# Memory query made turned at the head of the gate stage, another order of the first normed tiles, and the last output row by thirds

## The chip, the cores and the metric

The kernel runs on one core of a Trainium2 chip. The metric is the device time of one execution in microseconds (us). The engines are named as in the profile: PE (TensorE), with PEld its weight loads, DVE (VectorE), ACT (ScalarE), POOL (GpSimd), and SP (SyncE), which here only issues DMAs.

## The reference

One layer of a hybrid decoder for 1024 new-sequence tokens (`S`) and 8 sample tokens (`NB`), `T` = 1032 in all, width 1024. All is float32.

```
z = rmsnorm(x, norm1_g) @ w_in      # split: qa, ka, va (3 groups), qm, km, vm, om, gates, ga, gb
qm = qm * 64 ** -0.5                # the memory query, 512 columns
o_att = windowed, dilated attention of the groups (1, 4, 16), merged by their log-sum-exp
h_m   = mLSTM over chunks of tokens (qm, km, vm, input and forget gates), with a matrix state
x = x + (sigmoid(ga) * (o_att @ w_att_out) + sigmoid(gb) * ((sigmoid(om) * h_m) @ w_m_out)) @ w_o
y = x + (silu(h @ w_gate) * (h @ w_up)) @ w_down,   h = rmsnorm(x, norm2_g)
```

Besides y the outputs are the new key and value caches and the memory's states, for the sequence and for the samples (the latter from attention over their caches and one step of the memory).

## The kernel before

Every product is made of three, of high and low parts of both operands (`products`), as fp32r. `w_in` is taken in pieces of 128 rows by 512 columns: SP loads a piece into one of three `raw` buffers, POOL makes the high part `whi` and the low part `wlo` in a ring of 15 places, and the next load of a buffer waits for the low part. The first eight pieces are rounded by ACT (`round_weights`).

The program is a chain of blocks; each engine has a queue of its own in every block.

1. `project`: first the tokens are normed in tiles of 128 (`NormInput`): squares and root on ACT, the inverse on DVE, spread over the partitions by PE (`pe_norm`), then DVE scales the transposed tile in halves (`nrm`), ACT rounds it (`hi`) and DVE takes the rest (`lo`). `Projection` runs over 13 kinds of 512 columns (`KINDS`), nine units each: eight tiles of tokens (24 products of 128x512) and the samples' unit (16 products). A step u of all engines handles unit u and the tails of those before. Queries and keys are turned by PE two units later, copied by ACT, and stored by SP (`m_tr` and `a_tr`). Attention of group g takes two items for a tile of tokens (`Attention.at` says at which step), with products ahead of the softmax (`qk`), transposes and the products behind it (`pv`). `SampleScores`, from step `late` on, loads a cache tile and a query per step and reduces them on DVE; SP loads one step ahead.
2. `gate_projections`: 16 units of 128 gate columns by 1032 tokens, made already turned (weights stationary), in three segments of 344 tokens each (`segment_product`); ACT takes a segment into `sg` and stores a unit. From segment i = 3 (`FIRST`) on, `Chunks` runs the memory over eight chunks of tokens, five steps each, between the segments. `sp_init` loads the first two chunks.
3. `layer_end`: the output products, and the feed-forward part `Ffn`. Its last loop adds the products of `w_down` to `acc`, a row m of 128 columns at a time; PE turns a finished row (`turn`), ACT and DVE copy its halves, SP stores them. After the last row PE turns the new tokens' columns, and ACT and SP store them.

The order within a block is written out by hand. A block ends with an exit at the line of its `with` (L1139, L2248).

Of the kernel before, what the change touches and what calls it, by code (L numbers as in the profile page):

```python
# [12 lines left out]
F32 = mybir.dt.float32  # L13
# [5 lines left out]
P = 128  # L19
D = 1024  # L20
S = 1024
NB = 8
# [31 lines left out]
KINDS = [(0, 2), (0, 0), (1, 2), (0, 1), (1, 0), (1, 1), (2, 0), (2, 1), (2, 2)] + [("m", x) for x in range(4)]  # L54
# [60 lines left out]
def weight_pieces(t):  # L115
# [3 lines left out]
    cols += [CGA, CGA + 512, CGB, CGB + 512, COM, COM + 512]  # L119
# [251 lines left out]
class NormInput:  # L371
# [79 lines left out]

    def act_root(self, n):

# [5 lines left out]
        if n == 0:  # L459
            act.wait_ge(self.one, 1)  # L460
# [3 lines left out]
                       accum_out=self.ssq[0:rows, n:n + 1]).then_inc(self.sqd, 1)  # L464
        act.wait_ge(self.var, n + 1)
        act.activation(self.ssq[0:rows, n:n + 1], self.ssq[0:rows, n:n + 1], ACT.Sqrt).then_inc(self.std, 1)

    def act(self, n):
# [4 lines left out]
        rows, cols = self.rows(n), self.cols(n)  # L473
        for v in self.halves(n):
            act.wait_ge(self.nrm, v + 1)
            act.activation(core.xs[v % 2][:, 0, :, cols],
                           self.tmp[:, v % 2, :].rearrange("p (k c) -> p k c", k=4)[:, :, 0:rows],
                           ACT.Copy).then_inc(self.hi, 1)
# [21 lines left out]
    def dve(self, n):  # L500

        dve, core, ch = self.core.nc.vector, self.core, self.core.dve
        if not self.valid(n):
            return
        rows, cols = self.rows(n), self.cols(n)
        if n == 0:
            dve.memset(self.ssq[:], 1.0).then_inc(self.one, 1)
            dve.memset(core.hs[:].bitcast(F32), 0.0).then_inc(self.zero, 1)
        root = self.ssq[0:rows, n:n + 1]
        dve.wait_ge(self.sqd, n + 1)  # L510
        dve.tensor_scalar(root, root, 1.0 / D, EPS, ALU.mult, ALU.add).then_inc(self.var, 1)
        dve.wait_ge(self.std, n + 1)
        dve.reciprocal(root, root).then_inc(self.inv, 1)
        if n == 0:
            dve.wait_ge(self.g_in, 16)
# [3 lines left out]
        at = (n % 4) * P  # L519
        ch.link(dve.tensor_copy(self.rs[:, 0:rows], core.ps[:, 7, at:at + rows]))  # L520
        for v in self.halves(n):
            if v >= 2:
                dve.wait_ge(self.lo, v - 1)
            for k in range(4):
# [4 lines left out]
                if k < 3:  # L529
                    ch.mark(ins)  # L530
                else:
                    ch.wait()
                    ins.then_inc(self.nrm, 1)
# [3192 lines left out]
```

## Time and profile before

| | |
|---|---|
| median of 3 runs | 2161.61 us (2161.17 to 2162.16) |
| the profiled execution | 2158.37 us, span 2156.6 us |
| PE busy | 2117.9 us, 98% |
| PEld, DVE, ACT, POOL busy | 1977.4, 1066.8, 631.7, 715.7 us |
| DMA | 365.17 MB, mean 169 GB/s |
| median landing of a weight load of w_in, 256 KB | 4.2 us |
| median landing of a store of gates, 516 KB | 3.8 us |

A row of the timeline is start, duration, engine, line, operation, output<-input, and in brackets how long the engine was idle before and what ended that. A duration of a PE product includes its way through the array: products start closer together than that. SPq and ACTq rows are DMA issues.

### The profile page before, as it was taken

What the parts mean: (1) busy time and instruction counts of PE and PEld (TensorE: products, weight loads), DVE (VectorE), ACT (ScalarE), POOL (GpSimd) and SP (SyncE); (2) the same over time, 40 slices, a digit from 0 to 9 for tenths busy, and PEclk for the clock granted to TensorE, in tenths of its full rate; (3) what the DMA queues carried; (4) which work ended last, traced back from release to release, by engine and by line L of the source; (5) the groups of instructions that cost most, each with busy time, mean ns of one, the idle gap of its engine ahead of it and who ended that gap; (6) DMA issues with size and microseconds to landing.
All of it is one profiled execution on the core that took longest, in us unless ns stands there. A gap on an engine that the chain in (4) does not pass through costs nothing.

```text
span 2156.6 us, 36189 instructions
## 1 busy us (share of the span) xinstructions
PE 2117.9 (98%) x14248; PEld 1977.4 (92%) x14248; DVE 1066.8 (49%) x2112; ACT 631.7 (29%) x1354; POOL 715.7 (33%) x636
## 2 busy tenths in 40 slices
PE   7999999999999999999999999999999999999999
PEld 6788899999877778999989999999999999999998
DVE  5675777775233341233266544398454454442212
ACT  5221465544233232333211011143332332221001
POOL 3433321232112222222052334224544544554310
PEclk9999999999999999999999999999999999999999
DMA  6625534355548834545467641415545545387712
GB/s 201 210 101 170 176 117 144 131 187 174 180 154 286 271 132 149 165 148 162 134 214 239 207 154 54 148 60 180 183 150 178 182 151 178 105 329 288 259 41 79
DMA packets 233735, 365.17 MB, mean 169 GB/s; under 512 B 39222, under 2 KB 134262, under 8 KB 230870
## 3 DMA queue, kind: packets, MB, share of 16 engines
q1 hardware_dynamic: 211534, 317.48, 44.3%
q10 hardware_dynamic: 22032, 45.38, 6.1%
q8 instruction: 113, 1.85, 0.3%
q14 instruction: 56, 0.46, 0.1%
HBM read 276.19 MB, written 174.68 MB: 209 GB/s over the span
## 4 chain that ended last, share of the span: by engine, by line
PE 52%; DVE 5%; issue 2%; DMA 1%; ACT 1%; SPq 0%; DVEq 0%; ACTq 0%
PE ps L2855 20%; PE ps L2199 17%; PE ps L366 4%; PE ps L367 4%; PE ps L368 4%; PE ps L1637 1%; DMA h_mem<-c_ht 1%; DVE acc L3126 1%; PE ps L1412 0%; DVE x_a L2549 0%; PE ps L1629 0%; PE ps L1620 0%; PE ps L1646 0%; DVE x_c L2549 0%; DVE misc L3102 0%
## 5 line engine op out<-in xcount | busy, mean ns | idle before, releaser
L341 POOL CAST whi<-raw 128x512 fp32r<-128x512 f32 x228 | 167.6, 735 | 1046.1 <-PE ps L682 431.0
L343 POOL TENSOR_TENSOR wlo<-raw,whi 128x512 fp32r<-128x512 f32 x231 | 323.3, 1400 | 34.6 <-issue 10.3
L366 PE MATMUL ps<-whi,x_a 128*128 128x512 f32 x416 | 178.6, 429 | 0.0
L736 ACT ACTIVATE zt<-ps 128x512 f32<-128x512 f32 x104 | 62.1, 597 | 356.6 <-PE ps L368 302.6
L367 PE MATMUL ps<-wlo,x_a 128*128 128x512 f32 x416 | 166.5, 400 | 0.0
L368 PE MATMUL ps<-whi,x_a 128*128 128x512 f32 x416 | 166.5, 400 | 0.0
L366 PE MATMUL ps<-whi,x_b 128*128 128x512 f32 x416 | 166.0, 399 | 0.0
L368 PE MATMUL ps<-whi,x_b 128*128 128x512 f32 x416 | 166.0, 399 | 0.0
L367 PE MATMUL ps<-wlo,x_b 128*128 128x512 f32 x416 | 165.9, 399 | 0.0
L2855 PE MATMUL ps<-x_a,whi 128*128 128x258 f32 x960 | 156.2, 285 | 2.0 <-DVE acc L2657 1.8
L2855 PE MATMUL ps<-x_c,whi 128*128 128x258 f32 x960 | 154.5, 283 | 0.5 <-DVE acc L3334 0.5
L2199 PE MATMUL ps<-x_a,whi 128*128 128x344 f32 x792 | 148.2, 323 | 3.2 <-DVE x_a L2549 1.3
L3060 POOL TENSOR_TENSOR wlo<-wlo_f,whi 128x512 fp32r<-128x512 f32 x88 | 122.1, 1410 | 57.4 <-issue 39.1
L2855 PEld LDWEIGHTS ps<-x_a,whi 128*128 128x128 f32 x960 | 133.4, 191 | 2.6 <-DVE acc L2657 2.0
L2199 PEld LDWEIGHTS ps<-x_a,whi 128*128 128x128 f32 x792 | 129.0, 189 | 5.2 <-issue 5.1
L2855 PEld LDWEIGHTS ps<-x_c,whi 128*128 128x128 f32 x960 | 132.3, 190 | 0.8 <-issue 0.7
L3589 DVE TENSOR_TENSOR acc<-acc,ps 128x1032 f32<-128x1032 f32 x32 | 39.3, 1229 | 171.6 <-PE ps L2199 171.6
L982 DVE CUSTOM_DVE_ANT_0 sc<-ps,misc 128x128 f32<-128x128 f32 (+1 forms) x192 | 56.0, 348 | 120.9 <-PE ps L933 93.0
L368 PEld LDWEIGHTS ps<-whi,x_a 128*128 128x128 f32 x416 | 103.9, 250 | 10.4
L368 PEld LDWEIGHTS ps<-whi,x_b 128*128 128x128 f32 x416 | 103.5, 249 | 10.3
L367 PEld LDWEIGHTS ps<-wlo,x_b 128*128 128x128 f32 x416 | 103.4, 249 | 10.2
L366 PEld LDWEIGHTS ps<-whi,x_b 128*128 128x128 f32 x416 | 103.5, 249 | 9.9
(416 smaller groups left out, 4930.1 us busy)
## 6 DMA issues: line engine op xcount, KB each, us to landing
out<-in_cache_kv_w SPq DMA_DIRECT2D x144, 512.0 KB, 6.3
raw<-in_w_in SPq DMA_DIRECT2D x147, 256.0 KB, 4.2
a_tr<-tt SPq DMA_DIRECT2D x48, 256.0 KB, 2.0
out<-in_cache_kv_w SPq DMA_DIRECT2D x24, 508.0 KB, 5.5
raw<-in_w_down SPq DMA_DIRECT2D x44, 256.0 KB, 6.0
gates<-e_sg ACTq DMA_DIRECT2D x16, 516.0 KB, 3.8
rw<-gates ACTq DMA_DIRECT2D x16, 516.0 KB, 4.7
out<-zt SPq DMA_DIRECT2D x26, 256.0 KB
```

The lines of the kernel that those rows point to most:

```text
L341: pool.tensor_copy(self.whi[:, self.place(p), :], raw).then_inc(self.w_hi, 1)
L343: pool.tensor_tensor(self.wlo[:, self.place(p), :], raw, self.whi[:, self.place(p), :].bitcast(F32), ALU.subtract).then_inc(self.w_lo, 1)
L366: nc.tensor.matmul(out, lhs[0], rhs[0], start=start, stop=False)
L367: nc.tensor.matmul(out, lhs[0], rhs[1], start=False, stop=False)
L368: return nc.tensor.matmul(out, lhs[1], rhs[0], start=False, stop=stop)
L736: act.activation(self.zt[:, u % Z, :], ps[:, u % 2, :], ACT.Copy, scale=self.scale(u)).then_inc(self.ev, 1)
L982: ins = dve.tensor_tensor_reduce(self.sc[:, W % 2, 2 * par + j, 0:span], ps[:, 3 + par, 2 * j * P:2 * j * P + span], mask, SCALE, 3 * NEG, ...
L1637: last = pe.matmul(ps[:, bank, at], self.ww[:, self.at(h), :], self.v[:, b, h, :], start=True, stop=True)
L2199: last = nc.tensor.matmul(ps[0:m, bank + s, 0:SEG], w, x[:, s * SEG:(s + 1) * SEG], start=(k == 0 and i == 0), stop=(k == nk - 1 and i == 2))
L2855: last = core.nc.tensor.matmul(core.ps[:, bank + s, 0:Q], a, b[:, s * Q:(s + 1) * Q], start=start and i == 0, stop=stop and i == 2, skip_g ...
L3060: pool.tensor_tensor(core.wlo[:, at, :], self.source(c, x), core.whi[:, at, :].bitcast(F32), ALU.subtract).then_inc(core.a_lo, 1)
L3589: dve.tensor_tensor(seg3(acc[:, m, :]), seg3(acc[:, m, :]), self.res(n, m), ALU.add).then_inc(self.add[0], 1)
```

## The change

- The kind ("m", 0), the memory's query, leaves `KINDS` (12 kinds stay). Its columns stand first among the pieces of the gate stage, which has `U` = 20 units: four of the query (`QUERY`), copied with the scale, then the 16 of the gates. A query unit is stored by ACT with two DMAs: the tokens' part to `m_tr[0]` and the new tokens' part to `zm_s`, whose rows are tokens, so that each number goes to a place of its own. `FIRST` is 15 instead of 3. The first two chunks are loaded at i = 13, after SP has waited for all query stores.
- Group 2 of attention takes one item in each unit (before, two in three units). `late` is 78 instead of 81.
- At the start ACT makes a Sqrt of a constant, then the squares of tile 0 ahead of the first rounding; squares of tile 1, rounding and normed halves follow in another order, and DVE's order is written out in `dve_start`.
- The last row of the output is made in three segments of tokens, each with its own bank, addition and transposes; the row before is turned between them, as are the new tokens' columns, whose store goes ahead of the last row's.

```diff
-KINDS = [(0, 2), (0, 0), (1, 2), (0, 1), (1, 0), (1, 1), (2, 0), (2, 1), (2, 2)] + [("m", x) for x in range(4)]
+KINDS = [(0, 2), (0, 0), (1, 2), (0, 1), (1, 0), (1, 1), (2, 0), (2, 1), (2, 2)] + [("m", x) for x in range(1, 4)]
...
-    cols += [CGA, CGA + 512, CGB, CGB + 512, COM, COM + 512]
+    cols += [CQM, CGA, CGA + 512, CGB, CGB + 512, COM, COM + 512]
...
+    def act_first(self):
+
+
+        act = self.core.nc.scalar
+        act.wait_ge(self.one, 1)
+        act.activation(self.rs[:, 0:1], self.ssq[:, NT:NT + 1], ACT.Sqrt)
...
+    def act_square(self, n):
 
         act, core = self.core.nc.scalar, self.core
         if not self.valid(n):
             return
         rows, cols = self.rows(n), self.cols(n)
         act.wait_ge(self.x_in[n], 16)
-        if n == 0:
-            act.wait_ge(self.one, 1)
         spare = (core.xs[0][:, :, :, cols].rearrange("p a k c -> p (a k) c") if n < NT else
                  self.x[0:NB, 0, :].rearrange("p (k c) -> p k c", k=KD))
         act.activation(spare, self.rows_of(n).rearrange("p (k c) -> p k c", k=KD), ACT.Square,
...
+    def act_half(self, n, v):
+
+        act, core, rows = self.core.nc.scalar, self.core, self.rows(n)
+        act.wait_ge(self.nrm, v + 1)
+        act.activation(core.xs[v % 2][:, 0, :, self.cols(n)],
+                       self.tmp[:, v % 2, :].rearrange("p (k c) -> p k c", k=4)[:, :, 0:rows],
+                       ACT.Copy).then_inc(self.hi, 1)
...
+    def dve_start(self):
+
+
+        dve = self.core.nc.vector
+        dve.memset(self.ssq[:], 1.0).then_inc(self.one, 1)
+        dve.memset(self.core.hs[:].bitcast(F32), 0.0).then_inc(self.zero, 1)
+        self.dve_var(0)
+        self.dve_inverse(0)
+        dve.wait_ge(self.g_in, 16)
+        self.dve_factor(0)
+        self.dve_normed(0, 0)
+        self.dve_var(1)
+        self.dve_normed(0, 1)
+        self.dve_inverse(1)
+        self.dve_rest(0, 0)
+        self.dve_rest(0, 1)
+        self.dve_block(1)
...
-            return [core.m_tok[n, :, x - 1, :]] if x else []
+            return [core.m_tok[n, :, x - 1, :]]
...
+                at = g * (self.ITEMS + self.TAIL) + j
+                self.at[proj.unit(1, 0, 0) + (at * 3 // 2 if g < 2 else at + self.ITEMS + self.TAIL)] = (g, j)
         self.loads = {}
...
-        late = proj.unit("m", 0, 0)
+        late = proj.unit("m", 1, 0) - 3
...
+            norm.act_first()
+            norm.act_square(0)
             core.round_weights(0)
+            norm.act_sqrt(0)
+            norm.act_square(1)
             core.round_weights(1)
-            norm.act_root(0)
-            for p in range(2, 5):
+            core.round_weights(2)
+            norm.act_half(0, 0)
+            norm.act_sqrt(1)
+            norm.act_half(0, 1)
+            core.round_weights(3)
+            core.round_weights(4)
+            norm.act_keep(0)
+            core.round_weights(5)
+            norm.act(1)
+            for p in range(6, FIRST):
                 core.round_weights(p)
-            norm.act(0)
-            norm.act_root(1)
-            for p in range(5, FIRST):
-                core.round_weights(p)
-            norm.act_keep(0)
-            norm.act(1)
             norm.act_keep(1)
...
         def _(dve):
-            norm.dve(0)
-            norm.dve(1)
+            norm.dve_start()
...
-        self.load(0)
-        self.load(1)
...
-    U = 2 * KD
-    FIRST, PER, WIDE = 3, 6, 3
-    LOADS = {9: 0, 15: 1, 21: 2}
+    U, QUERY = 2 * KD + 4, 4
+    FIRST, PER, WIDE = 15, 6, 3
+    LOADS = {9: 0, 21: 1, 27: 2}
     p0 = core.taken
-    core.taken += 4 * KD
...
+        def stored(u):
+
+
+            return 16 * (u // 2) + 16 * min(u // 2, QUERY // 2)
+
         @block.sync
         def _(sp):
             chunks.sp_init()
             for i in range(3 * U):
                 core.load_weights(piece(i))
+                if i == FIRST - 2:
+                    for x in range(2):
+                        sp.wait_ge(out[x], stored(QUERY + x))
+                    chunks.load(0)
+                    chunks.load(1)
...
-                if i == FIRST:
+                if i == 3:
...
-                    act.wait_ge(out[u % 2], 16 * (u // 2))
+                    act.wait_ge(out[u % 2], stored(u))
                 wait_segment(core, act, i, p0, mm)
-                act.activation(sg[:, u % 2, s * SEG:(s + 1) * SEG], ps[:, i % 2, 0:SEG], ACT.Sigmoid).then_inc(ev, 1)
+                part = sg[:, u % 2, s * SEG:(s + 1) * SEG]
+                if u < QUERY:
+                    act.activation(part, ps[:, i % 2, 0:SEG], ACT.Copy, scale=SCALE).then_inc(ev, 1)
+                else:
+                    act.activation(part, ps[:, i % 2, 0:SEG], ACT.Sigmoid).then_inc(ev, 1)
                 if s == 2:
                     act.wait_ge(ev, i + 1)
-                    act.dma_start(core.gates[u], sg[:, u % 2, :]).then_inc(out[u % 2], 16)
+                    if u < QUERY:
+                        act.dma_start(core.m_tr[0, :, :, u * P:(u + 1) * P].rearrange("n p c -> p n c"),
+                                      sg[:, u % 2, 0:S].rearrange("p (n c) -> p n c", n=NT)).then_inc(out[u % 2], 16)
+                        with core.nc.allow_non_contiguous_dma(reason="queries of the new tokens"):
+                            act.dma_start(core.zm_s[:, u * P:(u + 1) * P].rearrange("b c -> c b"),
+                                          sg[:, u % 2, S:T]).then_inc(out[u % 2], 16)
+                    else:
+                        act.dma_start(core.gates[u - QUERY], sg[:, u % 2, :]).then_inc(out[u % 2], 16)
                 if step(i) is not None:
                     chunks.act(step(i))
             for i in range(2):
-                core.defer(out[i], 16 * U // 2)
+                core.defer(out[i], stored(U))
...
-            for half, done in enumerate((self.ya, self.yv)):
-                sp.wait_ge(done, k + 1)
+            if k == KD - 1:
+                sp.wait_ge(self.yn, 1)
+                sp.dma_start(o[1].rearrange("b s d -> (b s) d"), self.new).then_inc(self.new_out, 16)
+            for half in (0, 1) if k < KD - 1 else (1, 0):
+                sp.wait_ge((self.ya, self.yv)[half], k + 1)
                 sp.dma_start(y[k, half], self.turned(k, half).rearrange("p (n c) -> p n c", c=P)).then_inc(
                     self.out[k % 2], 16)
-        sp.wait_ge(self.yn, 1)
-        sp.dma_start(o[1].rearrange("b s d -> (b s) d"), self.new).then_inc(self.new_out, 16)
...
                 self.turn(m - 1)
-        self.turn(KD - 1)
-        for k in range(KD):
-            last = pe.transpose(ps[0:NB, k // 4, (k % 4) * P:(k % 4 + 1) * P], self.acc[:, k, S:T], core.ident[:])
-        last.then_inc(self.ytr, 1)
+        self.pe_last_row()
+
+    def pe_last_row(self):
+
+
+        pe, core, ps = self.core.nc.tensor, self.core, self.core.ps
+        (n, m), i = self.order[-1], len(self.order) - 1
+        tiles, p, cols = self.chunks[n], self.piece(n, m), slice(P * (m % 4), P * (m % 4) + P)
+        self.added(pe, i - 2)
+        for s in (2, 1, 0):
+            seg = slice(s * SEG, (s + 1) * SEG)
+            for k in range(len(tiles)):
+                (w_hi, w_lo), (hi, lo) = core.weight(p + k, cols), self.h_operand(tiles.start + k)
+                for j, (w, x) in enumerate(((w_hi, hi), (w_hi, lo), (w_lo, hi))):
+                    last = pe.matmul(ps[:, 3 + s, 0:SEG], w, x[:, seg], start=(k == 0 and j == 0),
+                                     stop=(k == len(tiles) - 1 and j == 2))
+            last.then_inc(self.mm[0], 1)
+            if s == 2:
+                self.turn(m - 1)
+            elif s == 1:
+                self.added(pe, i)
+                for k in range(KD):
+                    last = pe.transpose(ps[0:NB, k // 4, (k % 4) * P:(k % 4 + 1) * P], self.acc[:, k, S:T], core.ident[:])
+                last.then_inc(self.ytr, 1)
+                pe.wait_ge(self.yv, KD - 1)
+                self.turn_last(6, 8)
+        self.added(pe, i + 1)
+        pe.wait_ge(self.ya, KD - 1)
+        self.turn_last(3, 6).then_inc(self.ytr, 1)
+        self.added(pe, i + 2)
+        self.turn_last(0, 3).then_inc(self.ytr, 1)
+
+    def turn_last(self, first, last):
+
+
+        pe, core = self.core.nc.tensor, self.core
+        for n in range(first, last):
+            ins = pe.transpose(core.ps[:, 6 + n // 4, (n % 4) * P:(n % 4 + 1) * P],
+                               self.acc[:, KD - 1, n * P:(n + 1) * P], core.ident[:])
+        return ins
...
+    def dve_last_row(self):
+
+
+        dve, i, m = self.core.nc.vector, len(self.order) - 1, KD - 1
+        self.added(dve, KD * (len(self.chunks) - 2) + m)
+        for j, s in enumerate((2, 1, 0)):
+            dve.wait_ge(self.mm[0], self.mm[1] + i - i // 4 + j + 1)
+            part = self.acc[:, m, s * SEG:(s + 1) * SEG]
+            dve.tensor_tensor(part, part, self.core.ps[:, 3 + s, 0:SEG], ALU.add).then_inc(self.add[0], 1)
+            if s == 2:
+                self.dve_turned(m - 1, m)
+        self.dve_turned(m, KD + 1)
 
```

(Here and there the lines between are left out: `act_square`, `act_sqrt`, `dve_var`, `dve_normed` and the like are the bodies of the old `act_root` and `dve` cut into pieces.)

## Rows read from the trace of the kernel before

**Rows 1.** The page, busy time of PE.

```profile
PE 2117.9 (98%) x14248; PEld 1977.4 (92%) x14248; DVE 1066.8 (49%) x2112; ACT 631.7 (29%) x1354; POOL 715.7 (33%) x636
```

**Rows 2.** Waits of PE: us in total, times, longest us.

```profile
PE ps L2855 <- DVE acc L3323: 2.8, 1, 2.8
```

**Rows 3.** Timeline of ACT: a turned unit, a samples' unit, a segment.

```profile
185.21 0.59 ACT L738 ACTIVATE zh<-ps 8x512 f32<-8x512 f32 x1 [3.10 <-PE ps L682]
...
602.48 0.60 ACT L736 ACTIVATE zt<-ps 128x512 f32<-128x512 f32 x1 [2.48 <-PE ps L368]
...
608.51 0.60 ACT L736 ACTIVATE zt<-ps 128x512 f32<-128x512 f32 x1 [4.95 <-PE ps L368]
...
838.38 0.46 ACT L2308 ACTIVATE e_sg<-ps 128x344 f32<-128x344 f32 x1 [3.32 <-PE ps L368]
```

**Rows 4.** Timeline of PE, DVE, SP at the end of the projection.

```profile
823.90 0.40 PE L682 MATMUL ps<-wlo,hs 128*40 128x512 f32 x1
...
824.96 0.68 DVE L792 SCALAR_TENSOR_TENSOR zt<-ps,zh 8x512 f32<-8x512 f32 x1 [3.76 <-ACT zh L738]
...
826.00 0.33 SPq L310 DMA_DIRECT2D raw<-in_w_in  x1
...
826.78 0.40 PE L366 MATMUL ps<-x_a,whi 128*128 128x344 f32 x1 [2.48 <-PEq L1139]
```

**Rows 5.** Timeline of SP and DVE, a small sample unit.

```profile
783.71 0.30 SPq L1105 DMA_DIRECT2D k_qb<-z_s  x1
...
785.51 0.68 DVE L1123 TENSOR_TENSOR k_kc<-k_kc,k_qb 8x512 f32<-8x512 f32 x1 [1.27 <-DMA k_qb<-z_s]
```

**Rows 6.** Timeline of PE, first and tenth product (nine at that distance).

```profile
16.26 0.77 PE L366 MATMUL ps<-whi,x_a 128*128 128x512 f32 x1
...
20.25 0.49 PE L366 MATMUL ps<-whi,x_a 128*128 128x512 f32 x1
```

**Rows 7.** Timeline of SP, and DMA issues of 829 to 831.9 (KB, us to landing).

```profile
829.12 0.92 SPq L1599 DMA_DIRECT2D c_mb<-neg_all  x2
...
831.58 0.43 SPq L1605 DMA_DIRECT2D c_v<-m_tok  x1
...
c_v<-m_tok SPq DMA_DIRECT2D x1, 512.0 KB, 6.9
```

**Rows 8.** DMA issues of the whole span, and of 1061 to 1062.

```profile
h_mem<-c_ht SPq DMA_DIRECT2D x8, 512.0 KB, 7.0
...
x_t<-x_tt SPq DMA_DIRECT2D x2, 16.0 KB, 1.8
...
out<-c_state SPq DMA_DIRECT2D x2, 1.0 KB, 9.6
...
raw<-in_w_in SPq DMA_DIRECT2D x1, 256.0 KB, 8.4
```

**Rows 9.** Timeline of ACT, POOL, DVE at the start.

```profile
7.08 1.04 ACT L463 ACTIVATE x_a<-x_sb 128x1024 fp32r<-128x1024 f32 x1
...
10.39 1.28 POOL L343 TENSOR_TENSOR wlo<-raw,whi 128x512 fp32r<-128x512 f32 x1 [1.81 <-ACT whi L357]
...
10.89 0.29 DVE L520 COPY x_rs<-ps 128x128 f32<-128x128 f32 x1 [0.96 <-PE ps L449]
...
13.29 1.37 DVE L537 TENSOR_TENSOR x_a<-x_n,x_a 128x512 fp32r<-128x512 f32 x1
```

**Rows 10.** DMA issues of 0 to 2.3.

```profile
x_sb<-in_x_prompt SPq DMA_DIRECT2D x1, 512.0 KB, 6.3
...
g<-in_norm_g ACTq DMA_DIRECT2D x1, 4.0 KB, 7.4
```

**Rows 11.** Timeline of DVE, ACT, SP at the end.

```profile
2148.71 1.23 DVE L3589 TENSOR_TENSOR acc<-acc,ps 128x1032 f32<-128x1032 f32 x1 [4.70 <-PE ps L2199]
...
2151.79 0.60 ACT L3564 ACTIVATE raw<-ps 128x512 f32<-128x512 f32 x1 [1.61 <-PE ps L3470]
...
2153.70 0.30 SPq L3509 DMA_DIRECT2D out<-misc  x1
```

More of the change, by code:

```diff
@@ L472, in act @@
             return
-        rows, cols = self.rows(n), self.cols(n)
         for v in self.halves(n):
[L475 to L478, printed above, removed]
+            self.act_half(n, v)
         if n == NT:
@@ L498, in act_keep, with dve_var, dve_inverse, dve_factor @@
                            self.bank(v, rows), ACT.Copy).then_inc(self.xtd, 1)
[L500 to L509, printed above, removed]
+    def dve_var(self, n):
+        dve, root = self.core.nc.vector, self.ssq[0:self.rows(n), n:n + 1]
         dve.wait_ge(self.sqd, n + 1)
         dve.tensor_scalar(root, root, 1.0 / D, EPS, ALU.mult, ALU.add).then_inc(self.var, 1)
+    def dve_inverse(self, n):
+        dve, root = self.core.nc.vector, self.ssq[0:self.rows(n), n:n + 1]
         dve.wait_ge(self.std, n + 1)
         dve.reciprocal(root, root).then_inc(self.inv, 1)
[L514 to L515 removed]
+    def dve_factor(self, n):
+        dve, core, rows, at = self.core.nc.vector, self.core, self.rows(n), (n % 4) * P
         dve.wait_ge(self.rsp, n + 1)
@@ L518, in dve @@
             dve.wait_ge(self.nrm, 2 * n)
-        at = (n % 4) * P
-        ch.link(dve.tensor_copy(self.rs[:, 0:rows], core.ps[:, 7, at:at + rows]))
-        for v in self.halves(n):
-            if v >= 2:
-                dve.wait_ge(self.lo, v - 1)
-            for k in range(4):
-                ins = dve.scalar_tensor_tensor(self.tmp[:, v % 2, k * P:k * P + rows],
-                                               core.ps[:, 3 + v % 4, k * P:k * P + rows],
-                                               self.g1[:, 4 * (v % 2) + k:4 * (v % 2) + k + 1],
-                                               self.rs[:, 0:rows], ALU.mult, ALU.mult)
[L529 to L533, printed above, removed]
@@ L539, in dve, with dve_block @@
+    def dve_block(self, n):
+        self.dve_factor(n)
+        for v in self.halves(n):
+            self.dve_normed(n, v)
+        for v in self.halves(n):
+            self.dve_rest(n, v)
+    def dve(self, n):
+        dve, core = self.core.nc.vector, self.core
+        if not self.valid(n):
+            return
+        self.dve_var(n)
+        self.dve_inverse(n)
+        self.dve_block(n)
         if n == NT:
@@ L626, in valid @@
         return 0 <= u < self.units
-    def scale(self, u):
-        return SCALE if self.kind(u)[0:2] == ("m", 0) else 1.0
     def stores(self, u):
@@ L3520, in pe @@
                 self.products.total(3, self)
-        for i, (n, m) in enumerate(self.order):
+        for i, (n, m) in enumerate(self.order[:-1]):
             if i == 0:
@@ L3582, in dve @@
         self.dve_last(TILES - 1)
-        for i, (n, m) in enumerate(self.order):
+        for n, m in self.order[:-1]:
             self.complete(dve, n, m)
```

65 lines of the change are left out of this document (46 added, 19 removed).

## The prediction

> **What bounds the kernel now.** I read the head of the page first. TensorE (PE) is busy for 2117.9 of 2156.6 us [rows 1]. Next the waits of PE: the longest one after the start is 2.8 us [rows 2]. Inside the projection and gate stages I found no idle time of PE over 0.3 us except at their borders. So an edit there is worth the PE time that it takes away, as long as no other engine comes last, and each border is worth its own pipeline tail. Then I read the timeline around the three places that the diff touches. The profiled execution took 2158.37 us, 1.8 over its span; the sum below is a difference, and it is put on the median of the runs, 2161.61.
>
> **Part A, the memory query: PE work.** Removed from the projection are the nine units of kind (m, 0). A turned unit without attention follows the one before at 6.03 us (602.48 to 608.51), and a unit of the new tokens takes 3.70 us (ACT's 0.60 for the unit before and its 3.10 of waiting) [rows 3]. That makes 8 x 6.03 + 3.70 = 51.9 us. The attention of group 1, which ran beside them, falls beside (m, 1) now and costs PE what it did. Added are 4 x 3 segments in the gate stage at 3.77 us (0.46 of ACT, 3.32 of its waiting) [rows 3]: 45.2 us, with no transposes, since the query comes out turned. Difference **-6.7 us**. POOL splits eight pieces either way, and the first three segments' weights stand ready as those of the gates did.
>
> **Part A, the border.** The trace shows what ends a block: PE's last product starts at 823.90, ACT takes it, DVE adds it at 824.96, SP stores and issues one weight load at 826.00, and only then, at 826.78, does PE go on, released by line 1139, the block's end [rows 4]. So all engines meet there. Call PE's end E = 824.30. Before, the samples' steps (late = 81) ended at step 112, four before the last unit, and attention at 115. Now the units end at 107, the samples at 109, attention's last product in 107. Behind E then come in order: PE's last attention product (it was work before, too); DVE's L792 to E+1.3; DVE's copy of ot, 0.7, to E+2.0; SP, which stores the last unit before anything else in that step, then o_grp, then k_kc and k_qb of the last sample unit, whose issue starts at about E+2.8; it lands 1.8 later, as the row 783.71 to 785.51 shows [rows 5]; two DVE operations of 0.67; then 0.45 to the next block. PE goes on at E+6.4 to 6.5 in place of E+2.5, and 0.66 us of attention is done meanwhile: **+3.4 us**. Bounds: 1 if the sample loads go out early, 4 if SP is late.
>
> **Part A, the clock behind that gap.** PE is then idle for some 5.8 us. At the start, work after an idle stretch begins with 512-column products 0.43 apart (16.26 to 20.25, nine of them) and 0.23 after that [rows 6]: the level of 1.2 GHz, then that of 2.4, though the column of the granted clock says 1.00. The slow stretch costs 4.0 x (1 - 0.23/0.43) = 1.8 us. The gap of 2.8 us [rows 2] was not followed by one. I take the fall: **+1.8 us**, bounds 0 and 1.8. The Trainium skill (TensorE: Matmul & The Clock Gate, Part 1) says that an array left idle goes back to 1.2 GHz and rises only after sustained work; by that rule the 1.8 is due, and without it the sum would be 1.8 lower. The start of this trace agrees.
>
> **Part A, the first chunk's loads.** Chunk steps begin at i = 15 in place of 3, so they stand as far from the stage's end as before. But SP now waits at i = 13 for the query's stores. T is PE's end of segment 11. ACT takes the segment at T+0.3, issues the m_tr store at T+0.8 and the zm_s store at T+1.2. The loads of chunk 0 took from the first issue (829.12) to the landing of c_v, issued 831.58 and 6.9 on its way, 9.4 us [rows 7]. PE needs them after four more segments, T+15.1. So whatever the stores take beyond T+5.7 is PE's idle time. The m_tr store has the shape of h_mem (1024 pieces of 512 B), 7.0 us [rows 8]; stores of the same bytes in long pieces take 3.8 (table): T+4.6 to 7.8. The zm_s store is new in kind: 1024 pieces of 4 bytes. The trace bounds it from both sides [rows 8]: 1024 pieces of 32 B (x_t of the new tokens) land in 1.8 us, and 256 pieces of 4 B (c_state's column) in 9.6 us. The second row is the same pattern (neighbouring 4-byte words written by many partitions), and what is beside it speaks for a real cost: the weight load issued at 1061, 2.5 us behind them, needs 8.4 us [rows 8] where the median is 4.2 (table). I take 9.6: landing at T+10.8, PE waits 10.8 + 9.4 - 15.1 = **+5.1 us**. Bounds 0 and, at twice 9.6 each and one after the other, far above (below). A second fall of the clock would add 1.8; I leave it to the range. The Trainium skill (DMA: Bandwidth & Descriptors, Specifications) says that pieces under 512 B are read, modified and written. The 32-byte row disagrees as far as cost goes, the 4-byte row agrees; by the rule alone the stall would be there, by the 32-byte row alone not.
>
> **Part B, the start.** Nothing but DMA, ACT and DVE stands ahead of PE's first product at 16.26. Before, ACT rounds two pieces, then squares (7.08), loads a table of 1.28 us and takes the root, and DVE has the factor at 10.89 [rows 9]. Now the table is loaded while x is on its way, and the squares start when x has landed, at 5.2. Root at 6.9, inverse 7.1, PE's spread 7.3, which would put the factor at 8.2. But the gains land only at 1.14 + 7.4 = 8.54 [rows 10], so factor 8.6, first half normed at 10.0, second at 11.2. The second tile (landed 1.65 + 6.3 = 7.95) is squared at 8.0 to 9.2 and inverted after 11.2. The rests take 2 x 0.69, and 0.7 more where POOL is at work beside them as at 13.29: done at 12.8 to 13.5, PE starts near 13.6. The low halves follow at POOL's 1.28 each behind ACT's later roundings: numbers 6 and 7 are ready at 18.7 and 20.0, and PE asks for number 7 at 20.4. So **-2.6 us**; bounds -1.5 (a rest and a low half late) and -3.2. Every later unit of the first kind is chained to the one before, not to a fixed time, so the gain stays.
>
> **Part C, the end.** Before: add at 2148.71 for 1.23, PE turns, ACT copies at 2151.79, the new tokens' store goes last, issued at 2153.70 [rows 11]. Now PE does, from the row's start (2142.8, a row being 6.5 us with its turns), 36 products of 0.157 and 18 turns of 0.117, done at 2150.5; last add 0.5 to 2151.3, three turns, ACT's copy to 2152.6, last issue 2152.6 to 2153.1. The new tokens' store is out since 2149.7. Last issue 2153.1 in place of 2154.0: **-0.8 us**, bounds 0 and -1.2.
>
> **Sum.** -6.7 + 3.4 + 1.8 + 5.1 - 2.6 - 0.8 = +0.2, 2161.8 us. This is the forecast. Within 0.2% is 4.3 us to either side, about what a measurement of this kernel can tell from no change.
>
> **Rivals.**
> 1. The 4-byte store is cheap, like the 32-byte one. Then m_tr sets T+4.6 to 7.8 and PE waits 0 to 2. Sum -4.9 with the clock's fall, -6.7 without: 2154.9 to 2157.5. For it: the number of pieces alone costs nothing in rows 8. Against: the column store's row.
> 2. The store costs by the piece, so that 1024 take twice what 512 took or more (15 to 20 us), and the four follow each other through a stage of 45 us. The first is issued at 12.5 after the stage's start; at 15 each the last lands at 72.5, the loads at 81.9, and PE, due at 60.3, is 21.6 late: 21.6 in place of 5.1, 2178; at 20 each 2198. It decides for slower from 11 us a store on. For it: the whole queue crawls behind 512 such pieces. Against: the rows of zm_s lie further apart than the column's words.
> 3. The tail at the border is hidden after all (the sample loads out early, no fall of the clock), with the store cheap: -6.7 + 1 - 2.6 - 0.8 = -9.1, 2152.5.
>
> **How the numbers follow.** Forecast 0.37, its own range 2158 to 2167; rival 1 0.34; rival 2 0.20; rival 3 0.09. Faster by over 0.2%: 0.28 of rival 1 and all of rival 3, 0.37. Slower: rival 2 and 0.06 of the forecast, 0.26. Within: 0.37. The range reaches from 2153.5, in rival 3, to 2180, past the lower price of rival 2; less than a tenth lies outside below and about a tenth above.
>
> **What the profile after would show.** PE's first 128x512 product near 13.6, not 16.26. The gap at line 1139 near 6 us, with DVE's k_kc products inside it, and 344-column products some 0.29 apart behind it. A wait of PE at its first c_k, c_q product for a DMA, and the landing of zm_s<-e_sg in the list of issues: 2 us makes me wrong towards rival 1, 15 towards rival 2. SP's last issue at 2153.1 of the old time. I am wrong as a whole if the projection's units with attention in every one (7.4 us apart for group 2) show waits of PE.

## The result, and the profile after

The changed kernel takes 2195.01 us (median of 4 runs, 2194.24 to 2203.31) against 2161.89 (4 runs of the kernel before, 2161.17 to 2163.34): a ratio of 1.016, 95% interval 1.0145 to 1.0176. It is slower by 33 us. I had forecast 2161.8 with a range up to 2180. The profiled execution took 2194.30 us over a span of 2192.5, which is 35.9 more than that of the kernel before.

The page, and then the waits of PE (us in total, times, longest), show where to look. PE is busy 8 us more than in [rows 1], and it waits three times for a buffer of the query and once for the first chunk's loads. None of these four waits exists in the kernel before.

```profile
PE 2126.1 (97%) x14296; PEld 1993.5 (91%) x14296; DVE 1065.3 (49%) x2113; ACT 626.5 (29%) x1349; POOL 717.3 (33%) x636
...
PE ps L1679 <- DMA c_v<-m_tok: 11.7, 1, 11.7
PE ps L366 <- ACT e_sg L2377: 8.5, 2, 4.4
PE ps L366 <- PEq L1193: 5.6, 1, 5.6
...
PE ps L366 <- ACT e_sg L2379: 4.0, 1, 4.0
```

The timeline of ACT in the query stage tells what those waits are. After each pair of stores ACT has to wait, before it may overwrite the buffer of the unit two back, until that unit's zm_s store has landed:

```profile
794.82 0.60 ACTq L2386 DMA_DIRECT2D zm_s<-e_sg  x1
...
806.16 1.03 ACTq L2386 DMA_DIRECT2D zm_s<-e_sg  x1
816.73 0.81 ACT L2377 ACTIVATE e_sg<-ps 128x344 f32<-128x344 f32 x2 [11.00 <-DMA zm_s<-e_sg]
...
824.67 0.60 ACTq L2386 DMA_DIRECT2D zm_s<-e_sg  x1
834.89 0.81 ACT L2377 ACTIVATE e_sg<-ps 128x344 f32<-128x344 f32 x2 [10.65 <-DMA zm_s<-e_sg]
841.51 0.37 ACTq L2383 DMA_DIRECT2D m_tr<-e_sg  x1
841.91 2.81 ACTq L2386 DMA_DIRECT2D zm_s<-e_sg  x1
852.06 0.81 ACT L2379 ACTIVATE e_sg<-ps 128x344 f32<-128x344 f32 x2 [5.93 <-DMA zm_s<-e_sg]
...
864.84 0.46 ACT L2379 ACTIVATE e_sg<-ps 128x344 f32<-128x344 f32 x1 [6.19 <-DMA zm_s<-e_sg]
```

The landings are at 816.7, 834.9, 852.1 and 864.8. The first store, with none of its kind before it, lands 21.9 us after its issue. The others follow at 18.2, 17.2 and 12.8 us from each other. The DMA issues of the query stage (KB each, median us to landing), those of 794 to 795, and the bytes moved in 40 slices of 794 to 816 us say that the other transfers suffer too. The first m_tr store, with no zm_s store ahead of it, lands in 4.0; the three behind it take 18.9, 17.7 and 14.7. The weight loads of 256 KB issued from 794 to 816 take 18.6 at the median, where 4.2 is usual. The DMA engines look nearly fully busy while they move some 15 GB/s:

```profile
m_tr<-e_sg ACTq DMA_DIRECT2D x4, 512.0 KB, 16.2
...
zm_s<-e_sg ACTq DMA_DIRECT2D x4, 4.0 KB, 25.1
...
m_tr<-e_sg ACTq DMA_DIRECT2D x1, 512.0 KB, 4.0
...
zm_s<-e_sg ACTq DMA_DIRECT2D x1, 4.0 KB, 21.9
...
DMA  6869799995969599986789969985599939298557
GB/s 127 317 196 317 185 270 412 125 358 52 37 7 22 11 22 26 37 11 7 7 11 15 15 7 19 15 11 7 7 26 15 15 4 19 4 22 19 24 47 86
```

SP stood at its wait at i = 13 until the last landing. Its timeline and PE's show the loads of chunk 0 issued at 864.89 and PE's first product of the chunk 11.70 late (the loads of [rows 7] waited for no store):

```profile
864.89 0.91 SPq L1658 DMA_DIRECT2D c_mb<-neg_all  x2
...
873.76 2.08 PE L1679 MATMUL ps<-c_q,c_k 64*128 64x128 f32 x16 [11.70 <-DMA c_v<-m_tok]
```

From block to block the 35.9 us are made up so (start of the first product of a block, before and after): PE enters the gate stage at 826.78 and 779.94, 46.8 earlier. It leaves it at 1063.51 and 1096.71, 33.2 later, so the stage went from 236.7 to 316.8 us. After it 3.75 us are lost and 1.05 gained.

### The profile page after: what moved, and what is told of

Same layout as the page of the kernel before. It is cut to its first block, busy times and chain, and to the rows that moved or that the text cites. A ratio compares the mean times of both kernels' runs of the same rounds, so it can differ in the third digit from the quotient of the medians.

```text
span 2192.5 us, 36259 instructions
## 1 busy us (share of the span) xinstructions
PE 2126.1 (97%) x14296; PEld 1993.5 (91%) x14296; DVE 1065.3 (49%) x2113; ACT 626.5 (29%) x1349; POOL 717.3 (33%) x636
## 4 chain that ended last, share of the span: by engine, by line
PE 44%; DVE 4%; issue 1%; DMA 1%; ACT 0%; DVEq 0%; SPq 0%; ACTq 0%
PE ps L2933 23%; PE ps L2256 16%; PE ps L366 1%; PE ps L367 1%; PE ps L368 1%; PE ps L1471 0%; DMA v_hm<-h_mem 0%; DVE x_a L2627 0%; DMA rw<-hm_t 0%; DVE x_c L2627 0%; DVE misc L3180 0%; PE ps L3548 0%; PE ps L3631 0%; PE ps L2005 0%; DVE acc L2693 0%
## 5 line engine op out<-in xcount | busy, mean ns | idle before, releaser
L366 PE MATMUL ps<-whi,x_a 128*128 128x512 f32 x384 | 166.6, 434 | 1.5 <-DVE x_b L559 1.5
L367 PE MATMUL ps<-wlo,x_a 128*128 128x512 f32 x384 | 154.9, 403 | 0.0
L368 PE MATMUL ps<-whi,x_a 128*128 128x512 f32 x384 | 154.6, 403 | 0.0
L366 PE MATMUL ps<-whi,x_b 128*128 128x512 f32 x384 | 153.5, 400 | 0.2 <-POOL wlo L343 0.2
L367 PE MATMUL ps<-wlo,x_b 128*128 128x512 f32 x384 | 153.3, 399 | 0.0
L368 PE MATMUL ps<-whi,x_b 128*128 128x512 f32 x384 | 153.2, 399 | 0.0
L2256 PE MATMUL ps<-x_a,whi 128*128 128x344 f32 x792 | 148.4, 323 | 3.7 <-DVE x_a L3716 1.8
L789 ACT ACTIVATE zt<-ps 128x512 f32<-128x512 f32 x96 | 57.3, 597 | 320.4 <-PE ps L368 265.5
L366 PE MATMUL ps<-x_a,whi 128*128 128x344 f32 x324 | 112.6, 347 | 20.6 <-ACT e_sg L2377 8.5
L368 PEld LDWEIGHTS ps<-whi,x_a 128*128 128x128 f32 x384 | 98.5, 257 | 9.1
L366 PEld LDWEIGHTS ps<-whi,x_a 128*128 128x128 f32 x384 | 98.3, 256 | 9.4 <-DVE x_b L559 1.8
L367 PE MATMUL ps<-x_a,whi 128*128 128x344 f32 x324 | 106.4, 328 | 0.0
```

Source lines behind the costliest of these rows:

```text
L366: nc.tensor.matmul(out, lhs[0], rhs[0], start=start, stop=False)
L367: nc.tensor.matmul(out, lhs[0], rhs[1], start=False, stop=False)
L368: return nc.tensor.matmul(out, lhs[1], rhs[0], start=False, stop=stop)
L789: act.activation(self.zt[:, u % Z, :], ps[:, u % 2, :], ACT.Copy).then_inc(self.ev, 1)
L2256: last = nc.tensor.matmul(ps[0:m, bank + s, 0:SEG], w, x[:, s * SEG:(s + 1) * SEG], start=(k == 0 and i == 0), stop=(k == nk - 1 and i == 2))
```

## The experiments

The time in these runs scatters more than the ratios of the parts: the kernel before had medians of 2161.9 to 2162.8 and single runs from 2153.6 to 2172.6 there. So ratios are given with their intervals, and beside the time stands the length of the gate stage in the profiled execution, from PE's first product to its first of the next block: 236.7 us before, 316.8 in the change.

**Is it the store?** `q_none` leaves the second store out. The new tokens' query is missing from it; in its place in zm_s the projection stores their key once more. What differs in the gate stage, beside the count that ACT waits for:

```diff
-                        with core.nc.allow_non_contiguous_dma(reason="queries of the new tokens"):
-                            act.dma_start(core.zm_s[:, u * P:(u + 1) * P].rearrange("b c -> c b"),
-                                          sg[:, u % 2, S:T]).then_inc(out[u % 2], 16)
```

> The change without the second store of a query unit (the new tokens' query is left out; its place in zm_s is filled once, in the projection, with the new tokens' key). Theory S (the zm_s store of 4-byte pieces is what costs): in the changed kernel the gate stage takes 316.8 us where 236.7 + 45.2 = 281.9 were due, 34.9 too much, and all of it is behind this store. Without it PE's waits for e_sg (8.5 and 4.0) and for c_v (11.7) go, the m_tr store lands in 7 in place of 16.2 us, and the time is 2195.0 - 33 to 35 = 2160 to 2162. Rival M (the m_tr store of 512-byte pieces is slow by itself, and the other rides behind it): it still lands in 16 us, the waits stay, above 2185.

Measured: 2155.30 us, ratio 0.9974 (0.9958 to 0.999). The gate stage takes 284.8 us in place of 316.8 (PE's first product in it and behind it, below), the three waits for e_sg and the one for c_v are gone, and m_tr lands in 3.3. The stage gives back 32.0 us, in place of 33 to 35; the time fell by more, 39.7, and the 7.7 between them lie in places outside the stage that differ from one execution to the next (below). Theory S holds, rival M falls.

```profile
780.65 0.63 PE L366 MATMUL ps<-x_a,whi 128*128 128x344 f32 x1 [5.64 <-PEq L1193]
...
1065.43 0.40 PE L366 MATMUL ps<-x_a,whi 128*128 128x344 f32 x1 [1.32 <-PEq L2305]
```

**The bytes, the pieces, or their neighbours?** Six kernels keep a second store of the same 128x8 numbers and send it to a scratch tensor (as in the run before, the new tokens' query that is read later is replaced by their key). Their edits, a line of tensor and the store for each kind; the comments are mine:

```diff
+        self.q_s = dram("q_s", (4, P, NB))                # q_rows
+                        act.dma_start(core.q_s[u], sg[:, u % 2, S:T]).then_inc(out[u % 2], 16)
...
+        self.q_s = dram("q_s", (4, P, NB, 128))           # q_apart; 16 in pitch_64, 8 in pitch_32
+                            act.dma_start(core.q_s[u, :, :, 0:1], sg[:, u % 2, S:T].unsqueeze(2)).then_inc(out[u % 2], 16)
...
+        self.q_s = dram("q_s", (NB, 4 * P, 16))           # wide_64; 2 in wide_8
+                            act.dma_start(core.q_s[:, u * P:(u + 1) * P, 0:1].rearrange("b c a -> c b a"),
+                                          sg[:, u % 2, S:T].unsqueeze(2)).then_inc(out[u % 2], 16)
```

> The change with the second store writing the same 128x8 numbers to a scratch tensor whose rows are channels, 128 pieces of 32 bytes (what is read later is the stand-in of the run before it). Theory S: a store of 32-byte pieces lands in 2 us, as the 1024 such pieces of x_t do, and the time is that of the run without the store within 1 us, 2160 to 2163. Rival: any second small store on this queue costs its wait (two stores a unit, not their pieces): 2170 or more.

> The change with the second store still writing 1024 pieces of 4 bytes, but each 512 bytes from the next, to a scratch tensor. Theory P (the price is by the piece of 4 bytes, wherever it goes, 17 ns each): landing 17 to 25 us, the time is 2193 to 2197 like the change. Theory L (the price comes from several writers of the same line, since neighbouring channels of one token lie side by side): landing 2 to 4 us, 2160 to 2164.

> As the run with the pieces 512 bytes apart, but with 64 bytes from one 4-byte piece to the next (eight pieces in 512 bytes). Theory L512 (pieces within the same 512 bytes hold each other up): the store takes clearly longer than the 4.4 us it takes when they are 512 bytes apart, 8 us or more. Theory L64 (only a line of 64 bytes or less matters): 4.4 us, and the time is within 2 us of that run, 2155 to 2160.

> The same with 32 bytes from piece to piece, so that two pieces share 64 bytes. Theory L64: pairs hold each other up, landing above 4.4 us, toward 6 to 8. If 32 bytes is still free, landing 4.4 us, and the price needs closer neighbours than eight words (in zm_s they are one word apart).

> The change with the 4-byte pieces of the query written in zm_s's own order (a row for each token, channels side by side) but 64 bytes from channel to channel, to a scratch tensor. Theory L (several pieces in the same 64 bytes hold each other up; the order of the rows does nothing): landing 4 to 5 us, the time 2155 to 2162. Rival O (what made the runs with wide pieces cheap was their other order, all eight tokens of a channel next to each other, so that neighbours come from the same partition): landing 15 us or more, 2185 to 2197.

> The same with 8 bytes from channel to channel, so that 64 bytes hold pieces of eight partitions (in zm_s of sixteen). Theory L with a price by the neighbours in a line: between, landing 8 to 15 us, the time 2165 to 2185. If the price needs words that touch, 4 to 5 us.

The rows of DMA issues, one fence for each kernel in the order q_rows, q_apart, pitch_64, pitch_32, wide_64, wide_8:

```profile
q_s<-e_sg ACTq DMA_DIRECT2D x4, 4.0 KB, 3.2
```

```profile
m_tr<-e_sg ACTq DMA_DIRECT2D x4, 512.0 KB, 3.3
...
q_s<-e_sg ACTq DMA_DIRECT2D x4, 4.0 KB, 4.4
```

```profile
q_s<-e_sg ACTq DMA_DIRECT2D x4, 4.0 KB, 4.7
```

```profile
q_s<-e_sg ACTq DMA_DIRECT2D x4, 4.0 KB, 5.5
```

```profile
q_s<-e_sg ACTq DMA_DIRECT2D x4, 4.0 KB, 4.5
```

```profile
q_s<-e_sg ACTq DMA_DIRECT2D x4, 4.0 KB, 10.2
```

| kernel | pieces | from one to the next | landing | gate stage | time | ratio to before |
|---|---|---|---|---|---|---|
| the change | 1024 of 4 B | 4 B | 25.1 (the first 21.9) | 316.8 | 2195.01 | 1.016 (1.0145 to 1.0176) |
| wide_8 | 1024 of 4 B | 8 B | 10.2 | 292.3 | 2168.87 | 1.0032 (1.0017 to 1.0046) |
| pitch_32 | 1024 of 4 B | 32 B | 5.5 | 285.1 | 2158.04 | 0.9983 (0.9965 to 1.0001) |
| wide_64 | 1024 of 4 B | 64 B | 4.5 | 284.1 | 2160.72 | 1.0 (0.9985 to 1.0015) |
| pitch_64 | 1024 of 4 B | 64 B | 4.7 | 285.0 | 2162.42 | 0.9995 (0.998 to 1.001) |
| q_apart | 1024 of 4 B | 512 B | 4.4 | 284.6 | 2157.51 | 0.998 (0.9967 to 0.9993) |
| q_rows | 128 of 32 B | one block | 3.2 | 283.6 | 2159.20 | 0.999 (0.9974 to 1.0005) |
| q_none | none | | | 284.8 | 2155.30 | 0.9974 (0.9958 to 0.999) |

The number of pieces and their size stay the same in the first six rows of the table. What changes is the distance, and the landing falls from 21.9 us, with no store of the kind before it, to 4.4. So the price is that of separately written words that lie close together. From 64 bytes on it is gone, at 32 it is 1 us, at 8 it is 6, and at 4, where words touch, 17 to 18. wide_64 has zm_s's order of rows and is as cheap as pitch_64, so the order (rival O) does nothing. Theory P (17 ns a piece wherever it goes) falls. One thing beside the distance was not held fixed: the change alone writes to zm_s, the other kernels to a scratch tensor, and no run writes touching words there. wide_8, which lands 6 us later than the spread pieces in the same kind of scratch tensor, shows that close neighbours cost without zm_s; that the step from 8 to 4 bytes is all distance is not shown. What inside the memory path does this no run shows; that neighbours wait for each other is the name I give it.

Not all sizes came as expected. q_rows landed in 3.2 where 2 was expected, and q_apart in 4.4 where 2 to 4 was; pitch_32 shows the price of pairs, but at 5.5 and not 6 to 8. The times of wide_64 and pitch_64 are 5 and 7 us above q_none's, and pitch_64's is above its expected 2155 to 2160; their gate stages are as short as q_none's, so that is not the store. wide_8 lies where the expectation has it, with 7.5 us of stage lost for 10.2 of landing.

**Part B alone.** `start_only` is the kernel before with the new order of the start.

> The kernel before with part B alone (the order of the start). PE's first 128x512 product near 13.3 in place of 16.26 either way. Theory K (my prediction: the gain is kept): 2161.6 - 2.6 = 2159.0. Theory G (given back as in the trace of the change, where unit 5's copy waits for the a_v store until 62.00 and PE falls to the lower clock at 64 to 71, so that from unit 8 on all is 2.0 later): 2163.6. If the late landing of that one store was an accident of the profiled execution, theory K holds.

Measured: 2161.22 us, ratio 0.9992 (0.9979 to 1.0005): between the two theories and not told from no change. The traces tell more. First the DMA issue of the gains and PE's first 128x512 product in start_only, then the same in the changed kernel:

```profile
g<-in_norm_g ACTq DMA_DIRECT2D x1, 4.0 KB, 9.9
...
15.07 0.79 PE L366 MATMUL ps<-whi,x_a 128*128 128x512 f32 x1 [0.53 <-DVE x_b L559]
```

```profile
g<-in_norm_g ACTq DMA_DIRECT2D x1, 4.0 KB, 7.2
...
13.32 0.80 PE L366 MATMUL ps<-whi,x_a 128*128 128x512 f32 x1 [1.47 <-DVE x_b L559]
```

In the eleven traces that have part B with the gains issued second, they land after 7.1 to 7.5 us and the product is at 13.3 to 13.6 (once 14.6), or after 9.9 to 10.3 and it is at 15.1 to 15.5. Before part B the same late landing costs nearly nothing: end_only below has 10.0 and its first product at 16.50, against 16.26 at [rows 6]. So by these single traces part B makes the first product 2.9 us earlier when the gains are quick and 1.0 to 1.4 when they are not.

Theory G is half right. The loss at unit 5 is real where it occurs: ACT's copy of unit 5 follows that of unit 4 by 9.65 us in the changed kernel's timeline, because the a_v store lands late, where the kernel before needs 7.50 (54.93 to 62.43).

```profile
52.35 0.60 ACT L789 ACTIVATE zt<-ps 128x512 f32<-128x512 f32 x1 [4.20 <-DMA a_v<-zt]
62.00 0.60 ACT L789 ACTIVATE zt<-ps 128x512 f32<-128x512 f32 x1 [5.58 <-DMA a_v<-zt]
```

But start_only has 7.47, and end_only, without part B, has 9.21. Of the fourteen traces of this study six have 9.2 to 9.7 and eight 7.2 to 7.5. So it comes without part B too, and part B does not always bring it; whether part B makes it more frequent the traces don't tell. Five of the six are among the seven traces in which the gains land late, so the two may have one cause. No run tests that.

**The remedy.** `turned` is the whole change, but ACT puts the eight columns of each query unit into a tile, PE turns the four blocks after segment 12, and SP stores rows of 2 KB. `turned_early` moves the samples' steps too.

```diff
+                if u < QUERY and s == 2:
+                    act.activation(qs[:, u, :], ps[:, i % 2, SEG - NB:SEG], ACT.Copy, scale=SCALE)
...
+                if i == 3 * QUERY:
+                    pe.wait_ge(ev, 3 * QUERY)
+                    for u in range(QUERY):
+                        last = pe.transpose(ps[0:NB, 2, u * P:(u + 1) * P], qs[:, u, :], core.ident[:])
+                    last.then_inc(mm, 1)
...
+                    sp.dma_start(core.zm_s[:, 0:QUERY * P], qz[:]).then_inc(core.ml_in, 16)
...
-        late = proj.unit("m", 1, 0) - 3
+        late = proj.unit("m", 1, 0) - 6                   # turned_early
```

> The whole change, computing all outputs, with the new tokens' query gathered in a tile of 128x4x8, turned by PE (four transposes of 0.1 us after segment 12) and stored as 8 rows of 2 KB by SP. Theory S: time as without the store plus at most 1 us of PE, 2155 to 2160 on the chip of that run, 4 to 6 us below the kernel before there; ratio 0.997 to 0.999. Rival: the turned rows come too late or hold up SP's queue ahead of the chunks' loads, PE waits for c_v again, 2162 or more.

> The same with the samples' steps three units earlier (late = 75 in place of 78), so that the last one is done before the projection's last unit. My account of the border (the gap of 5.6 us at the projection's end is the last sample unit's loads and products behind the last unit): the gap falls to about 2.5 us, as in the kernel before [rows 4], and the time by 3 to 5 us against the run with late = 78 (3.1 of gap, 0 to 1.8 of clock). Rival (attention's tail, its copy of ot and the store of o_grp, sets the gap): it stays above 4.

Measured: turned 2159.56 us, ratio 0.9987 (0.9976 to 0.9997); turned_early 2156.28, ratio 0.997 (0.9959 to 0.9981). Both compute all outputs, and turned_early is 0.3% faster than the kernel before, clear of its interval. The border in three rows each, PE's first product of the gate stage, ACT's first copy of it, and PE's windows (start and end, length, busy times with counts of PE, PEld, DVE, ACT and POOL, granted clock, DMA share, GB/s), first turned, then turned_early:

```profile
775.45 0.63 PE L366 MATMUL ps<-x_a,whi 128*128 128x344 f32 x1 [5.62 <-PEq L1193]
...
782.02 0.46 ACT L2387 ACTIVATE e_sg<-ps 128x344 f32<-128x344 f32 x1 [12.15 <-PE ps L368]
...
775.40:778.00 2.60, 2.55 (x9) 2.58 (x10) 2.03 (x2) 0.00 (x0) 0.00 (x0) 0.50 0.01 3
```

```profile
777.63 0.40 PE L366 MATMUL ps<-x_a,whi 128*128 128x344 f32 x1 [2.62 <-PEq L1193]
...
783.23 0.46 ACT L2387 ACTIVATE e_sg<-ps 128x344 f32<-128x344 f32 x1 [8.18 <-PE ps L368]
...
777.60:780.00 2.40, 2.37 (x9) 2.40 (x10) 1.85 (x2) 0.00 (x0) 0.00 (x0) 0.57 0.55 162
```

The gap falls from 5.62 to 2.62 as my account of the border says; the rival (attention's tail) falls. The first segment takes 6.57 us after the long gap and 5.60 after the short one; in the kernel before (826.78 to 830.83) it took 4.05 at a granted clock of 1.00. So the lower clock costs 2.5 and 1.6 us. The length of a gap alone doesn't decide. The kernel before and end_only have the same gap of 2.48 us at this border: the granted clock is 1.00 behind it in the one (826.75 to 830.83) and 0.68 in the other, from 831.90 to 836.00:

```profile
831.90:836.00 4.10, 4.07 (x18) 4.10 (x19) 2.28 (x3) 1.27 (x1) 0.00 (x0) 0.68 0.33 94
```

Likewise, behind the 1.8 us in which PE waits for acc at the head of the feed-forward part (1345 to 1347 in the kernel before) the granted clock is 0.83 in the next ten microseconds there, and 1.00 in the changed kernel (1383.8 to 1393.8).

**Part C alone.**

> The kernel before with part C alone (the last output row by stretches of tokens). By the traces so far part C takes 0.7 us from the last addition on (my prediction: 0.8): ratio 0.9997, which so many rounds cannot tell from 1. Rival (PE's extra waits in the last row eat it): 1.000 to 1.001. In its trace the last SP issue should follow the last row but one's issue by 0.7 to 0.8 us less than in the kernel before [rows 11].

Measured: 2162.61 us, ratio 0.9997 (0.998 to 1.0014), as expected no verdict by time. By the trace the end of the span comes 11.8 us after the issue of the sixth row's store (2151.19 of 2163.0) where it was 12.9 (2143.68 of 2156.6). The issue in the kernel before, then in end_only:

```profile
2143.68 0.92 SPq L3506 DMA_DIRECT2D out<-raw  x2
```

```profile
2151.19 0.92 SPq L3509 DMA_DIRECT2D out<-raw  x2
```

The changed kernel has nearly the same: in its SP timeline, of a span of 2192.5, the issue and the last one of all are

```profile
2180.63 0.92 SPq L3587 DMA_DIRECT2D out<-raw  x2
...
2188.79 1.01 SPq L3587 DMA_DIRECT2D out<-raw  x2
```

or 11.9. Part C is worth 1.05 us in each, a little more than the 0.7 to 0.8 expected.

**Gains first.** turned_early with `norm.load_gains(act)` ahead of `norm.load(act, 0)`.

> The whole change with the query turned by PE and the samples three units earlier, and the load of the gains issued ahead of the first tile of x. In the traces with part B the gains (1024 pieces of 4 bytes, read) land after 7.1 to 7.4 us and PE's first 128x512 product is at 13.3 to 13.6, or after 9.9 to 10.3 and it is at 15.1 to 15.5. Theory Q (the gains wait behind the 512 KB of x): issued first they land by 5 us, DVE's factor no longer waits for them, and the first product comes at 12.6 to 13.4 every time; the median falls by 1 to 2 us against the run without. Rival (x now waits behind the small pieces): x lands 2 us later and the first product stays at 14 to 15.5.

Measured: 2155.90 us, ratio 0.9975 (0.996 to 0.9989), not to be told from turned_early. The gains land in 3.4 us, as theory Q has it, but PE's first transposes wait 7.0 us for x in place of 5.5, and the first product is at 14.03: the rival in the main. It takes away the bad case and spoils the good one.

## Why the prediction was wrong

| term | predicted | measured | from |
|---|---|---|---|
| removed units of (m, 0) | -51.9 | -52.0 | PE's last product 50.0 earlier, the start 2.0 later |
| border, gap of PE | +3.4 | +3.2 | 5.64 against 2.48 at [rows 4] |
| query's segments | +45.2 | +45.9 | stage of turned_early, 284.2 - 236.7 - 1.6, its four transposes included |
| clock behind the gap | +1.8 | +2.4 | first segment 6.41 (779.94 to 786.35) against 4.05 |
| stores and first chunk's loads | +5.1 | +31.8 | 316.8 - 236.7 - 45.9 - 2.4 |
| part B | -2.6 | -2.9, then +5.0 lost in units 5 to 8 | 16.26 to 13.32; from unit 8 on 2.0 later |
| behind the gate stage | 0 | +3.75 | a balance, see below |
| part C | -0.8 | -1.05 | end of the span |
| sum | +0.2 | +36 | spans: +35.9 |

The step that failed is "the first chunk's loads", in its price: "I take 9.6". I took the landing of c_state's column, 256 pieces, for 1024 pieces, and I let only the last store count. The traces show 21.9 us for the first store and 18.2, 17.2 and 12.8 more until the second, third and fourth have landed, so that the buffers stall PE three times (4.43, 4.07 and 4.00) before the loads stall it once (11.70). These are 24.2 us in place of 5.1. The other 7.6 of the row are left over by subtraction; the windows behind the border and behind the four stalls show that the granted clock is down after each of them, and I put the 7.6 down to that, 1.9 a stall:

```profile
779.90:786.40 6.50, 6.46 (x26) 6.49 (x27) 2.28 (x3) 0.05 (x1) 1.15 (x2) 0.60 0.00 1
...
817.30:821.30 4.00, 4.00 (x14) 4.00 (x15) 0.00 (x0) 0.24 (x1) 0.00 (x0) 0.50 0.70 73
835.40:839.40 4.00, 4.00 (x17) 4.00 (x18) 0.00 (x0) 0.29 (x1) 2.97 (x4) 0.62 0.11 6
852.60:856.60 4.00, 4.00 (x16) 4.00 (x17) 0.00 (x0) 0.26 (x1) 1.58 (x2) 0.60 0.11 2
873.80:877.80 4.00, 4.00 (x24) 3.78 (x25) 3.21 (x5) 2.45 (x8) 0.00 (x0) 0.56 1.12 338
```

The row that I used would have given nearly the right price by the piece. As rival 2 takes it, two stores of 256 in 9.6 us are 19 ns a piece, which is 19 us for 1024; this is an estimate, since the second was issued 1.9 us behind the first and two stores of 128 KB ran beside them. Rival 2 said "15 to 20 us" a store and "the four follow each other", 2178 to 2198, and the measured 2195 is in its range; I gave it 0.20. What I held against it, that the rows of zm_s lie further apart than the column's words, looked at the wrong distance. Within a row of zm_s the channels are words that touch, and that distance sets the price (wide_64 against wide_8 against the change). Rival 1's reason, that the number of pieces alone costs nothing, is no reason for this store, though q_apart nearly bears it out: 1024 pieces far apart land in 4.4, where the 128 of q_rows take 3.2. The row that it stood on was misread as well: a store of x_t is 16 KB, which is 512 pieces of 32 B, and not 1024. q_none is rival 1's case: its ratio is 5.6 us below the kernel before, and rival 1 has 4.9 to 6.7.

The Trainium skill (DMA: Bandwidth & Descriptors, Specifications) says that a transfer of under 512 B is a read-modify-write. In the prediction I read the column's row as agreeing with it. q_apart does not show such a cost: 1024 pieces of 4 bytes, each with 512 bytes to itself, land in 4.4 us. Here the size alone is not the price, the neighbours are.

The border and the fall of the clock were right in mechanism, and the sizes were near (3.2 for 3.4 and 2.4 for 1.8). What I took from [rows 2], that a gap of 2.8 us is not followed by a fall, does not hold in general: behind the same wait the granted clock is 1.00 in the kernel before (1482.5 to 1487.5) and 0.50 in the changed one (1516.5 to 1521.5). The work removed and added is right to 0.7 us, and inside the projection PE has no idle time over 0.3 us once the start is over, with an item of attention in each unit.

Part B's first product came 0.3 earlier than forecast. The reason "every later unit of the first kind is chained to the one before" was not enough for "the gain stays" in this trace. Unit 5's late store takes 2.2 us of it back. Most of the rest goes where the granted clock is 0.62 (64 to 68 us) and 0.53 (68 to 72), against 1.00 in the kernel before. end_only has the late store and such a fall without part B. As a mean, part B is probably worth less than 2.6 (start_only saved 1.7, with an interval from 1.1 lost to 4.5 saved), since the order now waits for the gains' landing, which in seven of the thirteen traces that issue them second comes 2.5 us or more later than the 7.4 of [rows 10].

Behind the gate stage I had put nothing. The 3.75 us are a balance, read by pairing PE's products of the two traces one by one. 4.3 are lost around the six copies of the merging coefficients, the granted clock's fall behind them (0.58 from 1119.7 to 1123.7) included. 2.8 are won: 1.5 where the clock of the kernel before fell behind the 1.8 us named above and this one's did not, 1.3 at a wait for DVE 100 us later. 2.6 are lost where the clock fell in this one and not in that (granted 0.56 from 1515 to 1520), and smaller pieces give back 0.35. The copies take 0.2 us each in the kernel before (1083.40) and up to 1.25 here. POOL's row, then DVE's:

```profile
1115.85 1.42 POOL L343 TENSOR_TENSOR wlo<-raw,whi 128x512 fp32r<-128x512 f32 x1 [7.67 <-issue]
...
1116.15 1.17 DVE L1432 COPY at<-ch 128x64 f32<-128x64 f32 x1
```

In the kernel before POOL starts its piece at 1084.37, behind the last copy. The copies take 1.15 us in all in the kernel before and in seven of the twelve experiments, 4.05 to 4.14 in the changed kernel and three of them, 2.7 to 2.9 in two. The Trainium skill (SBUF — State Buffer, Who interferes with whom) has an exclusive lock on a pair of ports that VectorE and GpSimd share; the rows agree, but no run was made on it, and why POOL is earlier in some traces stays open.

## What to carry to other kernels

Ask of every store how far apart two separately written words lie in the target. If a tensor is turned by the store itself, each word goes alone beside its neighbours, and 4 KB can hold up the transfers beside it for 17 us; turn it on PE, or leave 64 bytes between words. A price that one row of a trace gives for n pieces is a price by the piece until something excludes it, and four such stores behind a double buffer are paid four times. When a step is moved to a block's end, move the short chains of loads beside it as well: three units earlier took back 3 of the 5.6 us of idle time.

## What the runs showed of the hardware

- Stores of 1024 words land in 21.9 us (25.1 at the median when they queue) when the words touch, 10.2 at 8 bytes from one to the next, 5.5 at 32, 4.5 to 4.7 at 64 and 4.4 at 512. Behind a store of the first kind, 512 KB take 14.7 to 18.9 us in place of 3.3.
- The gains, 1024 words of 4 bytes read behind 512 KB of x, land after 7.1 to 7.5 or 9.9 to 10.3 us and nothing between, in thirteen traces. Issued first they take 3.4.
- After some 2 to 3 us of idle time the granted clock fell in some executions and not in others: behind 2.48 us it was 1.00 in the kernel before and 0.68 in end_only, behind 2.84 and 2.85 it was 0.50 and 1.00, behind 1.8 it was 0.83 and 1.00 (ten microseconds). Behind 5.6 us it was 0.50 for the next 2.6 us in all nine traces with that gap. A fall cost 1.5 to 2.6 us.
- Three such places (the gains' landing, one a_v store at the start, the copies beside POOL) move single executions of one kernel by 2 to 4 us each.
